# Attention steps of a four-layer model on one core: VectorE takes row maxima and level updates before it splits weights, and half of the heads' queries are turned in other banks

## The reference, cut to what matters

```python
proj = xn @ w_in[l]
(hq, hf, hi, hg, nq, kc, vc, ksl, vsl, ksw, vsw, ngate) = jnp.split(proj, ...)
o_hg = hgrn2_mixer(hq, hf, hi, hg, lb[l], hg_gnorm[l])       # a gated linear recurrence, 4 heads of 128
o_nsa = nsa_mixer(nq, kc, vc, ksl, vsl, ksw, vsw, ngate, ...)  # 8 query heads of 64, 2 key/value heads
h = h + jnp.concatenate([o_hg, o_nsa], -1) @ w_out[l]
```

## Time and profile before

| | |
|---|---|
| time, median of 3 runs | 1434.19 us (1428.82 to 1434.46) |
| the profiled execution's own time | 1422.43 us |
| its span, first to last instruction | 1420.6 us, mean granted TensorE clock 0.978 |
| busy: PE, PEld, DVE, ACT, POOL | 1349.1, 1143.8, 875.4, 713.6, 154.0 us |
| HBM traffic over the span | 157 GB/s |
| attention of layer 2, 714 to 826 us | PE busy 101.92 of 112 us, granted clock 0.91 |
| attention of layer 3, 1098 to 1209 us | PE busy 101.81 of 111 us, granted clock 0.92 |

### The profile page before, as it was taken

One profiled execution on the slowest core, in us unless ns is written; L12 is line 12 of the kernel. 1 busy time (PEld: TensorE's weight loads), 2 busy tenths in 40 slices (PEclk: granted clock), 3 DMA queues, 4 the chain that ended last, 5 costly groups with the idle time before them and its releaser, 6 DMA issues.

```text
span 1420.6 us, 18621 instructions
## 1 busy us (share of the span) xinstructions
PE 1349.1 (95%) x7251; PEld 1143.8 (81%) x7251; DVE 875.4 (62%) x1146; ACT 713.6 (50%) x1167; POOL 154.0 (11%) x176
## 2 busy tenths in 40 slices
PE   7879999999988999999989999999999999999998
PEld 5767888887877888888978878888888877788887
DVE  5875665656544666566855566666677646566665
ACT  6464554544464555456542445555465434455553
POOL 2211100012540400002101011000021010100000
PEclk9989999998999999999988999999999899999999
DMA  9433656545521555655631136555556211456661
GB/s 373 135 119 110 235 174 207 176 157 173 180 87 50 202 192 166 209 176 173 208 125 45 60 112 208 186 191 178 166 179 222 75 60 46 136 190 199 197 193 48
DMA packets 62329, 224.44 MB, mean 158 GB/s; under 512 B 7193, under 2 KB 7329, under 8 KB 62241
## 3 DMA queue, kind: packets, MB, share of 16 engines
q1 hardware_dynamic: 59616, 214.23, 45.4%
q0 software_dynamic: 1904, 6.82, 1.4%
q10 hardware_dynamic: 720, 2.19, 0.4%
HBM read 222.16 MB, written 1.05 MB: 157 GB/s over the span
## 4 chain that ended last, share of the span: by engine, by line
PE 76%; DVE 13%; ACT 5%; issue 3%; POOL 2%; DMA 0%; POOLq 0%; DVEq 0%; ACTq 0%
PE ps L323 15%; PE ps L277 14%; PE ps L282 14%; PE ps L281 14%; PE ps L327 7%; DVE wlo L1495 3%; PE ps L423 2%; PE ps L330 2%; PE ps L458 2%; PE ps L481 2%; PE ps L751 2%; ACT scr L987 1%; PE ps L329 1%; ACT whi L933 1%; DVE small L1580 1%
## 5 line engine op out<-in xcount | busy, mean ns | idle before, releaser
L1495 DVE TENSOR_TENSOR wlo<-raw,whi 128x1024 fp32r<-128x1024 f32 (+1 forms) x402 | 481.4, 1219 | 293.3 <-ACT whi L933 291.7
L933 ACT ACTIVATE whi<-raw 128x1024 fp32r<-128x1024 f32 (+1 forms) x409 | 424.2, 1048 | 314.2 <-PE ps L323 178.6
L323 PE MATMUL ps<-XT,whi 128*128 128x512 f32 x896 | 318.7, 399 | 0.0
L327 PE MATMUL ps<-XT,wlo 128*128 128x256 f32 x896 | 251.6, 281 | 0.0
L323 PEld LDWEIGHTS ps<-XT,whi 128*128 128x128 f32 x896 | 168.4, 188 | 41.1
L277 PE MATMUL ps<-whi,HT_hi 128*128 128x512 f32 (+1 forms) x496 | 188.2, 379 | 2.8 <-DVE wlo L1495 2.2
L282 PE MATMUL ps<-whi,HT_lo 128*128 128x512 f32 (+1 forms) x496 | 186.9, 377 | 0.0
L281 PE MATMUL ps<-wlo,HT_hi 128*128 128x512 f32 (+1 forms) x496 | 186.7, 376 | 0.0
L327 PEld LDWEIGHTS ps<-XT,wlo 128*128 128x128 f32 x896 | 169.2, 189 | 1.2
L277 PE MATMUL ps<-whi,XT 128*128 128x512 f32 (+2 forms) x352 | 142.3, 404 | 8.6 <-DVE wlo L1495 6.3
L281 PE MATMUL ps<-wlo,XT 128*128 128x512 f32 (+2 forms) x352 | 136.9, 389 | 0.0
(11 more groups left out here) (252 smaller groups left out, 1885.6 us busy)
## 6 DMA issues: line engine op xcount, KB each, us to landing
raw<-in_w_m SPq DMA_DIRECT2D x152, 512.0 KB, 4.2
raw<-in_w_n SPq DMA_DIRECT2D x108, 512.0 KB, 4.4
raw<-in_w_c SPq DMA_DIRECT2D x48, 512.0 KB, 4.3
raw<-in_w_o SPq DMA_DIRECT2D x32, 512.0 KB, 3.6
raw<-in_w_kv SPq DMA_DIRECT2D x16, 512.0 KB, 4.5
raw<-in_w_b SPq DMA_DIRECT2D x16, 512.0 KB, 3.4
raw<-in_w_w SPq DMA_DIRECT2D x16, 512.0 KB, 4.9
raw<-in_w_a SPq DMA_DIRECT2D x12, 512.0 KB, 7.3
```

The costliest lines, as they stand in the source:

```text
L323: m = pe.matmul(outs[f][:, :], hi[:, j, at], both, start=(k == 0), stop=False)
L327: pe.matmul(outs[f][:, 0:T], lo[:, j, at], XT[0][:, k, :], start=False, stop=False)
L933: act.activation(whi[:, g % NSPLIT, 0:w], raw[:, g % NRAW, 0:w], ACT.Copy).then_inc(split_hi, 1)
L1495: dve.tensor_tensor(wlo[:, g % NSPLIT, 0:w], raw[:, g % NRAW, 0:w], whi[:, g % NSPLIT, 0:w].bitcast(F32), ALU.subtract).then_inc(split_lo, 1)
```

## The change

Four edits.

1. In `soft` on DVE the maximum of a step no longer has splits ahead of it (`full(..., 0)`: only units that TensorE needs in order to close that bank). The splits that it did before now come after the step's `between` work.
2. In `advance(l)` the splits ahead of the wait for level l-1 are cut to what TensorE needs to close it, `take` has none, and the remaining ones come at the end of `advance`.
3. Heads 4 to 7 of the queries are turned in banks 2 and 3. TensorE starts scores(0) once the keys and heads 0 to 3 are copied out. It then issues the first woven tile, which so moves from behind scores(1) to ahead of it, and waits for heads 4 to 7 behind that tile.
4. `hgrn_out(0)` moves on TensorE from ahead of values(5) to behind it, the compressed scores move by one place each, and `hgrn_out(1)` moves into step 8. ACT's and DVE's parts of it move one step later.

```diff
-            def attend(tags, specs, between, turn_banks=(6, 7), weave=None):
+            def attend(tags, specs, between, turn_banks=(6, 7), weave=None, first=None):
...
                 scores(0)
+                if first:
+                    first()
...
-                    if s < 2:
+                    if s < 2 and (n, s) != (0, 0):
                         next(tiles_left, None)
...
-                            turn(f"zT{L}.{tt}.{g}", 6 + tt, tiles)
+                            turn(f"zT{L}.{tt}.{g}", (2, 3)[tt] if g == 1 else 6 + tt, tiles)
...
                 for tt in range(TT):
-                    for g in range(3):
-                        read_out(f"zT{L}.{tt}.{g}")
+                    read_out(f"zT{L}.{tt}.2")
+                    read_out(f"zT{L}.{tt}.0")
                 pe.wait_ge(ev("masked"), L)
+
+                def other_heads():
+                    next(tiles_left)
+                    for tt in range(TT):
+                        read_out(f"zT{L}.{tt}.1")
...
-                     (6, 1): lambda: level(8), (6, 2): lambda: hgrn_out(0),
-                     7: lambda: cmp_scores(0), (7, 1): lambda: cmp_scores(1), (7, 2): lambda: hgrn_out(1),
+                     (6, 1): lambda: level(8), 7: lambda: hgrn_out(0),
+                     (7, 1): lambda: cmp_scores(0), (7, 2): lambda: cmp_scores(1), (8, 1): lambda: hgrn_out(1),
...
-                     12: hgrn_rows}, (6, 6), weave)
+                     12: hgrn_rows}, (6, 6), weave, other_heads)
...  ScalarE's soft
-                      7: lambda: hgrn_in(0), 8: lambda: (cmp_exps(), hgrn_in(1)),
+                      8: lambda: (hgrn_in(0), cmp_exps()), 9: lambda: hgrn_in(1),
...  VectorE's soft
-                    ps = full(f"{tag}.s{i}")
+                    ps = full(f"{tag}.s{i}", 0)
...
                     m.then_inc(ev("maxed"), 1)
+
+                    st["cap"] = fills[...s of step n + 1].pos + AHEAD if n + 1 < len(steps) else len(units)
                     if n in between:
-
-                        st["cap"] = fills[...s of step n + 1].pos + AHEAD if n + 1 < len(steps) else len(units)
                         between[n]()
-                        st["cap"] = len(units)
+                    splits(fills[f"{tag}.s{i}"].pos + AHEAD)
+                    st["cap"] = len(units)
...  take, advance
-                    ps = full(f"lev{L}.{l}")
+                    ps = full(f"lev{L}.{l}", 0)
...
-                    splits(f.pos + AHEAD)
+                    splits(f.need)
                     dve.wait_ge(bank_full[f.bank], f.turn)
...
                     if l < LEVELS:
                         dve.tensor_tensor(decay_of[l], ...)
+                    splits(f.pos + AHEAD)
...
-                            9: lambda: (cmp_probs(), branch(2, 0), hgrn_sums(0), hgrn_sums(1)),
+                            9: lambda: (cmp_probs(), branch(2, 0), hgrn_sums(0)),
+                            10: lambda: hgrn_sums(1),
```

More of the change, by code:

```diff
@@ L1585, in soft @@
                     m.then_inc(ev("maxed"), 1)
+                    st["cap"] = fills[f"{steps[n + 1][0]}.s{steps[n + 1][1]}"].pos + AHEAD if n + 1 < len(steps) else len(units)
                     if n in between:
-                        st["cap"] = fills[f"{steps[n + 1][0]}.s{steps[n + 1][1]}"].pos + AHEAD if n + 1 < len(steps) else len(units)
                         between[n]()
-                        st["cap"] = len(units)
+                    splits(fills[f"{tag}.s{i}"].pos + AHEAD)
+                    st["cap"] = len(units)
             def weights_of(tags, tag, tt, gate=None):
```

## The result

The changed kernel takes 1411.07 us (median of 4 runs, 1406.15 to 1411.7) where the kernel before takes 1434.28 (4 runs, 1428.82 to 1434.46): ratio 0.984, 95% interval 0.9808 to 0.9872, 23 us less. In a later session, beside variants, it was 1410.0 against 1432.37, ratio 0.9856 [0.9825, 0.9888]. The profiled execution of the changed kernel took 1406.15 us (span 1404.4, mean granted clock 0.985), that of before 1422.43.

What follows compares the result with a forecast made beforehand. TensorE, busy 95%, was taken as the bound, through its pauses behind DVE and its lower clock. Gains of 10.9 and 13.0 us (-24), less 5 for the clock, gave -19 from the median 1434.2: 1415, range 1407 to 1430.

Steps and rivals of the forecast that it cites:

- the prediction's sums: Gains at full clock in the attention stages: 13.0 us in layer 2 and 10.9 in layer 3, together 24.
- Edit 3, start: At scores(0): TensorE runs 1.1 us ahead, mostly not kept; level 2 gains 0.25 us (layer 3), 1.1 (layer 2), waiting about 2.2.
- Level 3: DVE waits only for level 2, so level 3 starts earlier: 2.8 us gained in layer 3, 3.6 in layer 2.
- Levels 3 to 6: This span takes 18.2 us instead of 25.14 (layer 3) and 26.46 (layer 2): 7.0 and 8.3 us gained.
- `hgrn_out(0)`: TensorE's 1.67 us wait before it goes through edit 4, `take(8)` being done right behind level 8: 1.7 us gained per layer.
- The tail: At the last step, DVE's split comes behind the maximum of scores(11), in front of the gates: 0.6 us lost per layer.
- What the clock takes back: Lower clock likely behind level 2 for 3 to 14 us; 7 us taken, costing 2.5 us per layer, 5 in all.
- B: Rival, chance 0.20: stall moves to level 2, slow stretches keep their length, only waits are gained: -7 us, 1427.
- C: Rival, chance 0.09: no change, since ACT sets the pace and the time reappears at the next turn; 1432.
- D: Rival, chance 0.09: slower, clock falls at level 2 and stays at 1.2 GHz through levels 3 to 8; 1438 with 55 us slow.

Runs made afterwards that it cites:

- pairs and threes: Kernels with edits 1, 2; 1, 2, 4; 1, 2, 3; and 2, 3, each against the kernel before: ratios 0.9888, 0.9867, 0.9879 and 0.988.

## Why the prediction was right, and where not

**The size.** 1415 was predicted, 1411 measured. In the pair of profiles the layers gained 9.9 and 8.1 us up to the output projection, where the prediction's sums less 2.5 are 10.5 and 8.4. That these agree so well is in part chance: in the second profile the two layers gained 6.3 and 7.2.

**Edit 3, start: right in its place, small in size.** Scores(0) starts 1.2 us earlier; level 2 stands at 21.06 instead of 21.68 and 22.55, 0.6 and 1.5 us kept (0.25 and 1.1 predicted). The wait there is 1.52 and not 2.2. The prediction credits this to edit 3, and its estimate of ACT's order holds only because edit 1 takes DVE's splits from in front of the maximum of step 1. Without edit 1, edit 3 makes level 2 later by up to 1.6 us.

**Level 3: right.** At full clock 4.67 us behind level 2 (second profile, layer 3, where 4.6 was predicted; 4.66 with edit 2 alone), 5.71 where the slow stretch lies over it.

**Levels 3 to 6: right.** 18.45 us against 18.2, with 0.49 for the new wait before level 4 (0.8) and 4.10 for level 5 to 6 (4.0). In the execution where the slow stretch lasted 17 us it was 22.94.

**`hgrn_out(0)`: the time came, the reason was wrong.** Of the step "`take(8)` is done right behind level 8, and values(5) now stands in front", the second half does nothing. Edit 4 alone leaves 0.84 of the 1.67 us; every kernel with edit 2 has no wait there, in the old place too. The earlier trace rows had said so: the split at 1167.01 stood in front of `take(8)`, and it is edit 2 that moves it. The 1.7 us belong to edit 2, and edit 4's are 0 within what was measured.

**The tail: mis-sized.** "0.6 us lost" is exact for the delay (6.89 to 7.50) and leaves out what follows. Edits 1 and 4 lengthen the wait from 0.63 to 1.24 and 1.77, and the lower clock came behind it in 9 of the 12 layers profiled with the longer waits, for 6.8 us each time, against 2 of 16 with 0.63, for 3.4 us. Half of 6.8 in three of four layers is 2.5 us a layer that the 0.6 does not hold. The step looked for the clock's answer only at the longest wait, and not at one that the change made longer.

**"What the clock takes back": right on average behind level 2, by luck as a whole.** Behind level 2 the slow stretches of the changed kernel are 3.4 and 3.4 us, then 17.1 and 0: 6 on average where 7 was taken. To this come the tail and step 8. Of the first profile's 20 us of slow stretches 13.6 are of these two unforeseen kinds, 6.8 us of time; in the second it is about 20 of 37.6. So the profiled executions are 16.3 us apart, 2.7 less than predicted. The medians are 23 apart, 7 more than the profiles, because the median run of before lies 11.8 us above its profile and that of the changed kernel only 4.9. Setting a difference of profiles against the median assumed that these two are the same. The two errors have opposite signs, and 1415 comes within 4 us of 1411 by that luck.

**The rivals.** B (the stall moves to level 2 and the slow stretches stay) is half seen in the execution with 17 us behind level 2, and then only in one layer; that execution is 9.7 us ahead of the profile of before, near B's 7. The condition that B names, a slow stretch that needs a tile to end, fits where the stretches of before ended, but tiles ran inside them as well (the 4.94 us of the earlier trace rows), so a tile does not by itself end one. C is out: the waits went, and no wait of a level names ACT. D is out by 27 us. One sum of the prediction is a little low: the ten waits of the earlier trace rows add up to 15.1 us, not 14; nothing of the forecast rests on it.

The Trainium skill ("TensorE: Matmul & The Clock Gate", section "What's actually happening") has the throttled state as the default and activity as what releases it. The traces agree in direction at one place at a time, with the numbers of the last section: longer waits bring the lower clock more often. That a longer wait before level 2 brings it every time was the prediction's own conclusion, and the traces do not bear it out: at 1.4 to 1.5 us it came in 13 of 18 layers. The same section says that one kernel shows a differing number of slow matmuls from run to run, and here the traces agree: 3.4, 17.1 and 0 us at one place.

**Open.** Why the clock falls in step 8 or just ahead of it, 64 to 77 us behind the last turn of the queries, where PE shows no wait in the 4 us before. It is not edit 4: with edits 1 and 2 together, with or without 4, it falls there in 8 of 10 layers, with edit 2 and not 1 in 3 of 10, without edit 2 in 1 of 8. So it goes with edit 1 beside edit 2; how, is not shown, and no run tried it by itself. Whether the small differences between the pairs and threes are real is open as well.

## What to carry to other kernels

Work out for each edit alone which instruction in the trace it moves: when one group of lines stood in front of three waits, the edit that moves it has all three, and the others need a reason of their own. A short wait that an edit makes longer is to be priced with the clock that may fall behind it, wherever it stands, and not by its own length. Two edits that each shift an engine's order can spoil each other or need each other (3 without 1: level 2 later by 1.6 us; 1 alone: slower), so run them apart.

## What the runs showed of the hardware

At one place of the kernel, a longer wait of TensorE brings the lower clock more often; at another place the same length can bring it always or never. This is counted over fourteen profiles (before, the changed kernel twice, edit 2 twice, nine others), two layers each; a wait counts as followed when the lower clock begins inside it or at most 4 us behind it.

| place | wait, us | followed by the lower clock |
|---|---|---|
| before level 2 | none | 0 of 4 layers |
| | 0.70, 0.71 | 0 of 2 |
| | 1.37 to 1.52 | 13 of 18 |
| | 3.74 | 4 of 4 |
| before level 3 | 0.49 to 0.52 | 2 of 8 |
| | 1.40 to 3.00 | 6 of 6 |
| before level 6 | 1.45 to 1.55 | 3 of 8 |
| before `hgrn_out(0)` | 1.67 to 1.69 | 0 of 6 (in two it begins over 5 us behind) |
| before the `hr` turns | 0.63 to 0.65 | 2 of 16 |
| | 1.23 to 1.77 | 9 of 12 |

So the length of a wait alone does not tell, and in step 8 the clock falls without one. The same kernel at the same place may show 3.4, 17.1 or 0 us of it (the changed kernel, level 2), so that one profile does not tell a typical clock: runs of one program on one chip differed by 13 us with their mean granted clock (0.970 to 0.977).
